# Sums of squares of the retention outputs: rounded high and low parts in place of plain fp32 products

## What is computed

```python
def retention_chunk(S, q, k, v):                      # for each of 4 heads: DK = 256, DV = 512
    scores = einsum('bihd,bjhd->bhij', q, k) * decay
    intra = einsum('bhij,bjhe->bihe', scores, v)
    cross = einsum('bihd,bhde->bihe', q, S) * q_decay
    S_new = exp(lg * C) * S + einsum('bjhd,bjhe->bhde', k * k_decay, v)
    return intra + cross, S_new

def retention_out(o, gate, w_out):
    o = o * rsqrt(mean(o * o, axis=-1) + EPS)         # over the 512 values of a head
    return (silu(gate) * o) @ w_out
```

## Time and profile before

| | |
|---|---|
| median of 3 runs | 2008.25 us (2007.5 to 2014.1) |
| span of the profiled execution | 2016.3 us (no separate time of it is listed) |
| TensorE busy | 1926.1 us, 96% |
| VectorE busy | 1033.0 us, 51% |
| ScalarE busy | 692.8 us, 34% |
| GpSimd busy | 440.1 us, 22% |
| mean granted clock of TensorE | 0.984 |
| TensorE's wait for `sample_state` loads (line 953) | 7.5 us in 4 waits |
| TensorE's wait for sample-state updates (line 989) | 3.4 us in 4 waits |

### The profile page before, as it was taken

One profiled execution on the slowest core, in us unless ns is written; L12 is line 12 of the kernel. 1 busy time (PEld: TensorE's weight loads), 2 busy tenths in 40 slices (PEclk: granted clock), 3 DMA queues, 4 the chain that ended last, 5 costly groups with the idle time before them and its releaser, 6 DMA issues.

```text
span 2016.3 us, 35504 instructions
## 1 busy us (share of the span) xinstructions
PE 1926.1 (96%) x14783; PEld 1775.5 (88%) x14783; DVE 1033.0 (51%) x1170; ACT 692.8 (34%) x898; POOL 440.1 (22%) x106
## 2 busy tenths in 40 slices
PE   7999999999999999999999999799997999999998
PEld 6969969969889999999999999655555999999998
DVE  4445245245436865555532535466665466646462
ACT  4132232232224325252531432243545332515241
POOL 2302312312303312121133233000000332121212
PEclk9999999999999999999999999998998999999999
DMA  5341441441243222222232221688998222322231
GB/s 162 126 155 55 137 142 68 137 140 63 101 167 95 84 70 99 84 83 83 98 94 64 65 84 44 206 242 242 286 282 247 85 84 68 101 84 86 80 104 47
DMA packets 197347, 239.11 MB, mean 119 GB/s; under 512 B 16418, under 2 KB 168354, under 8 KB 197026
## 3 DMA queue, kind: packets, MB, share of 16 engines
q1 hardware_dynamic: 175650, 183.27, 30.0%
q10 hardware_dynamic: 21488, 53.46, 8.0%
q0 software_dynamic: 80, 0.52, 0.1%
HBM read 210.77 MB, written 26.12 MB: 117 GB/s over the span
## 4 chain that ended last, share of the span: by engine, by line
PE 64%; issue 16%; DVE 6%; DMA 5%; POOL 4%; ACT 2%; SPq 2%; ACTq 1%; DVEq 0%; POOLq 0%
PE PS L801 12%; PE PS L802 11%; PE PS L803 11%; POOL w_lo L741 4%; PE PS L817 4%; PE PS L819 4%; PE PS L818 4%; DMA k_page<-in_cache_k 3%; PE PS L880 3%; PE PS L881 3%; PE PS L882 3%; SPq L683 1%; DVE k_page_t L2390 1%; PE PS L1363 1%; PE PS L1318 1%
## 5 line engine op out<-in xcount | busy, mean ns | idle before, releaser
L741 POOL TENSOR_TENSOR w_lo<-w_raw,w_hi 128x2048 fp32r<-128x2048 f32 (+2 forms) x101 | 438.9, 4346 | 1545.0 <-ACT w_hi L1468 1545.0
L1468 ACT ACTIVATE w_hi<-w_raw 128x2048 fp32r<-128x2048 f32 (+2 forms) x101 | 178.1, 1764 | 640.8 <-PE PS L803 415.5
L801 PE MATMUL PS<-hidden_hi,w_hi 128*128 128x296 f32 (+1 forms) x1024 | 304.4, 297 | 0.7 <-DVE hidden_tmp L2159 0.6
L803 PE MATMUL PS<-hidden_hi,w_lo 128*128 128x296 f32 (+1 forms) x1024 | 304.7, 298 | 0.0
L802 PE MATMUL PS<-hidden_lo,w_hi 128*128 128x296 f32 (+1 forms) x1024 | 304.2, 297 | 0.0
L801 PE MATMUL PS<-x_hi,w_hi 128*128 128x296 f32 (+1 forms) x896 | 269.9, 301 | 5.7 <-DVE x_lo L1918 2.8
L802 PE MATMUL PS<-x_lo,w_hi 128*128 128x296 f32 (+1 forms) x896 | 268.7, 300 | 0.0
L803 PE MATMUL PS<-x_hi,w_lo 128*128 128x296 f32 (+1 forms) x896 | 268.0, 299 | 0.0
L880 PE MATMUL PS<-w_hi,x_hi 128*128 128x256 f32 x800 | 225.8, 282 | 0.4 <-DVE fox_gate L2311 0.4
L882 PE MATMUL PS<-w_lo,x_hi 128*128 128x256 f32 x800 | 224.8, 281 | 0.0
L881 PE MATMUL PS<-w_hi,x_lo 128*128 128x256 f32 x800 | 224.6, 281 | 0.0
(11 more groups left out here) (306 smaller groups left out, 3883.4 us busy)
## 6 DMA issues: line engine op xcount, KB each, us to landing
w_raw<-in_w_mlp_up SPq DMA_DIRECT2D x32, 1024.0 KB, 5.3
w_raw<-in_w_mlp_down SPq DMA_DIRECT2D x32, 1024.0 KB, 5.0
k_page<-in_cache_k SPq DMA_DIRECT2D x256, 128.0 KB, 5.9
v_page<-in_cache_v ACTq DMA_DIRECT2D x56, 512.0 KB, 8.3
w_raw<-in_w_ret_in SPq DMA_DIRECT2D x24, 1024.0 KB, 5.4
sample_state<-in_state_ret SPq DMA_DIRECT2D x32, 512.0 KB, 5.6
out_state_ret_sample<-sample_state ACTq DMA_DIRECT2D x32, 512.0 KB, 4.3
w_raw<-in_w_ret_out SPq DMA_DIRECT2D x16, 512.0 KB, 3.4
```

Of the source, the lines that this page charges most:

```text
L741: pool.tensor_tensor(lo, raw, hi.bitcast(F32), ALU.subtract).then_inc(lo_done, 1)
L801: pe.matmul(o, wh[:, w], xh[:, t, cols], start=(t == 0), stop=False)
L803: last = pe.matmul(o, wl[:, w], xh[:, t, cols], start=False, stop=(t == kt - 1))
L1468: act.activation(part(WH[n.slot], n, kt), part(WR[n.slot], n, kt), ACT.Copy).then_inc(hi_done, 1)
```

## The change

The squares are split: ScalarE writes them twice, rounded into `SQH` and plain into `TT4`; VectorE takes `TT4 - SQH` into `SQL` (`squares_low`); TensorE multiplies ones of type fp32r with the four pieces of `SQH`, waits for `SQL`, and multiplies with its four pieces, into the same bank. `squares_low(1)` stands on VectorE ahead of `new_state(4)`, `squares_low(0)` between `new_state(6)` and `new_state(7)`. `SQL` and `SQH` lie where the head's `Q` and `K` lay, which are no longer needed by then. The ones leave the constants and are written by GpSimd at the start into `ONR`; the plain sums elsewhere read that tile as fp32.

```diff
-KEEP, KEEP_N = columns([("ident", P), ("ones", P), ("eps", 1), ("one", 1)])
+KEEP, KEEP_N = columns([("ident", P), ("eps", 1), ("one", 1)])
...
+        ONR, at = place("ones_r", [P, P], at, F32R)
...
+        SQ_AT = R2 + (4 * RET_N + 31) // 32 * 32
+        SQL, at2 = place("o_squares_lo", [P, 4, HF], SQ_AT, F32R)
+        SQH, _ = place("o_squares_hi", [P, 4, HF], at2, F32R)
...
+            pool.memset(ONR[:].bitcast(F32), 1.0).then_inc(ones_set, 1)
...
             def sum_squares(hf, h):
 
-                pe.wait_ge(osq_done, 2 * h + 2 - hf)
+                pe.wait_ge(osq_done, 4 * h + 3 - 2 * hf)
                 pe.wait_ge(o_evac, 5 * h + 4)
                 for v in range(4):
-                    last = pe.matmul(PS[:, 4 + hf, 0:HF], ck("ones"), TT4[:, v, :], start=(v == 0), stop=(v == 3))
+                    pe.matmul(PS[:, 4 + hf, 0:HF], ONR[:], SQH[:, v, :], start=(v == 0), stop=False)
+                pe.wait_ge(osq_low, 2 * h + 2 - hf)
+                for v in range(4):
+                    last = pe.matmul(PS[:, 4 + hf, 0:HF], ONR[:], SQL[:, v, :], start=False, stop=(v == 3))
                 last.then_inc(osq_used, 1)
...
+            pe.wait_ge(ones_set, 1)
             qkv(Blk(0), first_tiles, sums=0)
...
                 def squares(hf):
-                    act.activation(TT4, O[:, :, HF * hf:HF * hf + HF], ACT.Square).then_inc(osq_done, 1)
+                    half = O[:, :, HF * hf:HF * hf + HF]
+                    act.activation(SQH[:], half, ACT.Square).then_inc(osq_done, 1)
+                    act.activation(TT4, half, ACT.Square).then_inc(osq_done, 1)
...
+                def squares_low(hf):
+                    dve.wait_ge(osq_done, 4 * h + 4 - 2 * hf)
+                    dve.tensor_tensor(SQL[:], TT4, SQH[:].bitcast(F32), ALU.subtract).then_inc(osq_low, 1)
+
...
-                for b in range(4, DB):
+                squares_low(1)
+                for b in range(4, 7):
                     new_state(b, 0 if b % 2 == 0 else 6)
+                squares_low(0)
+                new_state(7, 6)
```

More of the change, by code:

```diff
@@ L83, in constants @@
     put(keep, KEEP, "ident", np.eye(P))
-    put(keep, KEEP, "ones", np.ones((P, P)))
     put(keep, KEEP, "eps", np.full((P, 1), EPS))
@@ L384, in program @@
         x_turned = sem("x_turned")
+        ones_set = sem("ones_set")
         x_built = sem("x_built")
@@ L424, in program @@
         osq_used = sem("osq_used")
+        osq_low = sem("osq_low")
         oroot_done = sem("oroot_done")
@@ L905, in norm_sum @@
                     c = slice(a + w * i, a + w * i + w)
-                    last = pe.matmul(PS[:, 4 * n.slot + i, HF:HF + w], ck("ones"), RR[:, c], start=False, stop=True,
+                    last = pe.matmul(PS[:, 4 * n.slot + i, HF:HF + w], ONR[:].bitcast(F32), RR[:, c], start=False, stop=True,
                                      skip_group_check=True)
@@ L910, in norm_sum @@
                         last = pe.matmul(PS[:, 4 * n.slot, HF + SW + w:HF + SW + w + 1], RR[:, a:a + P],
-                                         ck("ones")[:, 0:1], start=False, stop=True, skip_group_check=True)
+                                         ONR[:, 0:1].bitcast(F32), start=False, stop=True, skip_group_check=True)
                 last.then_inc(sums_ready, 1)
@@ L1148, in fox_sums @@
                     for hf in range(2):
-                        pe.matmul(PS[:, 3 + 4 * hf, 0:HF], ck("ones"), RR[:, HF * hf:HF * hf + HF], start=True, stop=True)
+                        pe.matmul(PS[:, 3 + 4 * hf, 0:HF], ONR[:].bitcast(F32), RR[:, HF * hf:HF * hf + HF], start=True, stop=True)
                     for w, (a, _) in enumerate(WINDOWS):
-                        last = pe.matmul(PS[:, 3, HF + w:HF + w + 1], RR[:, a:a + P], ck("ones")[:, 0:1], start=False,
+                        last = pe.matmul(PS[:, 3, HF + w:HF + w + 1], RR[:, a:a + P], ONR[:, 0:1].bitcast(F32), start=False,
                                          stop=True, skip_group_check=True)
```

## The result

The changed kernel takes 2020.97 us (median of 5 runs, 2019.35 to 2022.9) against 2008.25 (5 runs, 2007.31 to 2014.1). The ratio is 1.0052, with a 95% interval of 1.0034 to 1.0071. The prediction was 2009.3 with a range to 2015: the time lies outside, on the slow side.

The account below looks back on a forecast made before the run. TensorE, busy 1926.1 of 2016.3 us, was taken as the bound. Second calls +0.14, start -0.17 and clock +1.0 summed to +1.0 us, carried over to the median 2008.25: 2009.3 us, range 2003.5 to 2015.

Parts of the forecast that it names:

- part 4: Behind the second call: VectorE's last state update, store, root and output scaling come later, nobody waits soon; cost nothing.
- part 5: Kernel start: ones leave the constants, 64 KB less in the first transfer; taken at -0.17 us.
- part 6: TensorE's granted clock at the heads' ends: idle grows, work shrinks; taken at +1.0 us, a third of one fall.
- part 3: Second call, low half waiting on VectorE's subtraction: heads 1, 3 each 0.67 us later, heads 0, 2 earlier; sum +0.14 us.
- rival 1: Heads' ends: clock falls in heads 1 and 3 too, heads 0 and 2 start units at half clock; +9.6 us, chance 0.10.

Follow-up runs that it names:

- split_first: The changed kernel's split in the first call of each head alone, the second call summing plain squares as before; ratio 1.0023 to the kernel before, +4.2 us.
- high_only: The changed kernel with the low part left out (one Square, no subtraction, no wait, four one-pass products per call); ratio 1.0017 to the kernel before, +3.6 us.

## Why the prediction was wrong

**Right.** The subtraction takes 1383 to 1393 ns in all eight cases (line 2043); 1380 was taken from the earlier trace rows. The products take one pass each. The low parts hold the second call, as their subtraction stands on VectorE behind the update of state 6, and the pause is 1.22 us where the high products run at full clock (head 2); at half clock they take longer, and it is 0.29, 0.29 and 0.79 us in heads 0, 1 and 3, so not the 1.2 to 1.5 of every head. The head's end at full clock takes 8.91 us where the sum gave 8.35 + 0.67 = 9.02. The low part of the first call ends ahead of the transfer. Nothing waits for what is delayed behind (part 4), and the start gives nothing that can be seen (part 5).

**Wrong: part 6, the clock term.** It was taken at +1.0 us and is about +10: the mean clock falls from 0.985 to 0.977, some 60 us at half clock become 92, and 32 x 0.33 us is 10.6. With 2.3 us from the second calls, where part 3 had +0.14, that is 12.9, and 11.6 +- 3.2 was measured. This was rival 1, put at 2018 and given one chance in ten. Its sign came true, as all four heads lose clock, but its parts only roughly: it had 3.0 us more for each of heads 1 and 3, and the profiles show 4.3 and 3.1 more in head 1 and 1.2 in head 3, so the nearness of its 9.6 us is in part luck. Three errors made its chance so small. First, I costed the first call at nothing, as the transfer covers it; its work also helps to keep the clock up through that wait (falls at the transfer in 13 of 24 heads' ends without it, in 1 of 40 with it), and `split_first` has the price, 4.2 +- 2.7 us. Second, I priced the gains of heads 0 and 2 as if half clock were a fixed backdrop against which shorter work pays (part 3, -1.2 us), but the time at half clock isn't fixed: head 0 came out at 12.62 and 10.83 us, where 11.33 - 0.22 was expected. Third, I read from one execution that two heads of four fall and took that for a fixed pattern; a second profile of the same kernel has falls in other heads (the first table), and this profile was itself 10 us above the median. I also took both falls to stand behind the transfer wait, at head 0's price of 2.98 us; head 2 fell only at the pause ahead of state 7 and lost 2.50.

The rule of the Trainium skill's "TensorE: Matmul & The Clock Gate", part 1, that I weighed in part 6 was the better guide: activity releases the throttle. By it, a change that takes activity away can only lose clock. The trace agrees, with 0.96 for 0.99 over the retention layer. The section "HAM oscillation" on the same page of the Trainium skill warns of short matmul bursts between waits on transfers of some 3 to 5 us. The heads' ends here are of that kind, but the waits are shorter: in the changed kernel's heads none is longer than 2.8 us, and the clock fell all the same.

**Wrong: TensorE's busy time.** It rose by 5.1 us (3.5 in the second profiles) in place of falling by 6 to 9, for the same reason: the records of the work at half clock are longer.

**Open.** How much activity is needed, and where, isn't settled: `high_only` and the changed kernel lose about the same clock (0.9776 and 0.9773), so putting the low products in behind a pause wins none back, but no run here separates their timing from their amount, nor missing work from the longer pause that it leaves. The fox layer, whose products no kernel changed, ran at 0.91 to 0.96 in the profiles (1170 to 1560 us), without a pattern that I could tie to a kernel. The loss of the changed kernel is placed in the retention layer by two profiles; that of the kernels with the change in one call, with one profile each, is not.

## What to carry to other kernels

Where TensorE stands between short waits, its work has two prices: the time it takes, and the clock that it keeps up. Here, cutting work ahead of a wait that is there anyway saved nothing and could cost the clock in all that follows the wait; before such a change, look at the granted clock in each such place over several executions. Price a fall by the stretch behind it, and if a cut is wanted all the same, try cheap products in the gaps beside it. They gave the changed kernel 14 us, and the kernel before nothing that could be measured.

## What the runs showed of the hardware

A program on one core, unchanged, spread over 22 us in 120 runs (2002 to 2024), and the mean granted clock of a run accounts for two thirds of the variance (correlation -0.82). Matmuls whose results nobody reads made a kernel faster: 29 products in each of four heads' ends, 13.7 us. Leaving out half the work of the sums of squares in the kernel before lowered its mean clock from 0.985 to 0.981.
